# One subtraction of 2048 columns on GpSimd where there were four of 512

## The reference

```python
for layer in range(2):
    h = _rmsnorm(x, norm_mix[layer])
    if layer == 0:
        q, k, v, g, alr, u, sv = _split(h @ even_w_in[0], EVEN_SPLITS)
        m = concat([_gla(q, k, v, g, alr, ...), _sgu(u, sv, ...)])
        x = x + m @ even_w_out[0]
    else:
        p = h @ odd_w_in[0]
        m = concat([_rwkv7(p[..., :RWKV_IN], ...), _conformer_conv(p[..., RWKV_IN:], ...)])
        x = x + m @ odd_w_out[0]
    f = jnp.square(jax.nn.relu(_rmsnorm(x, norm_ffn[layer]) @ w_up[layer]))
    x = x + f @ w_down[layer]
return _rmsnorm(x, norm_final)
```

## Time and profile before

| | |
|---|---|
| median of 3 runs | 1486.62 us |
| lowest and highest | 1486.29 and 1496.51 us |
| the profiled execution, its own time | 1486.62 us |
| its span in the profile | 1484.8 us |
| TensorE (matmul) busy | 1400.2 us, 94% |
| VectorE busy | 683.8 us, 46% |
| ScalarE busy | 420.8 us, 28% |
| GpSimd busy | 514.5 us, 35% |
| mean granted TensorE clock | 0.954 |

### The profile page before, as it was taken

One profiled execution on the slowest core, in us unless ns is written; L12 is line 12 of the kernel. 1 busy time (PEld: TensorE's weight loads), 2 busy tenths in 40 slices (PEclk: granted clock), 3 DMA queues, 4 the chain that ended last, 5 costly groups with the idle time before them and its releaser, 6 DMA issues. The chain is left out here.

```text
span 1484.8 us, 18004 instructions
## 1 busy us (share of the span) xinstructions
PE 1400.2 (94%) x7124; PEld 1138.8 (77%) x7124; DVE 683.8 (46%) x972; ACT 420.8 (28%) x535; POOL 514.5 (35%) x383
## 2 busy tenths in 40 slices
PE   4999998999999999889999999998799999999997
PEld 3896976888888888668878778686577888888886
DVE  6234356641024412666758677665556430044213
ACT  4545322321122212353324232221323321222210
POOL 3442342554444544241111110110043554454541
PEclk9999998999999999899999996996898999999998
DMA  4320212223223222111010000000021323223221
GB/s 185 125 97 29 74 68 85 85 85 114 85 85 109 88 90 108 57 57 58 1 58 29 29 29 1 29 29 0 0 86 59 111 85 113 85 85 113 85 85 57
DMA packets 16792, 106.01 MB, mean 71 GB/s; under 512 B 1872, under 2 KB 2144, under 8 KB 4704
## 3 DMA queue, kind: packets, MB, share of 16 engines
q1 hardware_dynamic: 15872, 103.83, 19.7%
q10 hardware_dynamic: 864, 1.36, 0.3%
HBM read 103.09 MB, written 2.10 MB: 71 GB/s over the span
## 5 line engine op out<-in xcount | busy, mean ns | idle before, releaser
L411 POOL TENSOR_TENSOR w_lo<-w_raw,w_hi 128x512 fp32r<-128x512 f32 x376 | 509.9, 1386 | 933.6 <-ACT w_hi L477 324.7
L749 PE MATMUL ps<-h_hi,w_hi 128*128 128x512 f32 x792 | 322.2, 407 | 7.9 <-DVE h_lo L1191 4.3
L749 PE MATMUL ps<-h_hi,w_lo 128*128 128x512 f32 x792 | 312.3, 394 | 0.0
L749 PE MATMUL ps<-h_lo,w_hi 128*128 128x512 f32 x792 | 312.2, 394 | 0.0
L749 PEld LDWEIGHTS ps<-h_hi,w_hi 128*128 128x128 f32 x792 | 150.8, 190 | 54.8 <-issue 18.4
L477 ACT ACTIVATE w_hi<-w_raw 128x2048 fp32r<-128x2048 f32 x58 | 111.1, 1915 | 276.5 <-PE ps L749 204.2
L749 PEld LDWEIGHTS ps<-h_hi,w_lo 128*128 128x128 f32 x792 | 150.8, 190 | 32.4
L749 PEld LDWEIGHTS ps<-h_lo,w_hi 128*128 128x128 f32 x792 | 151.1, 191 | 30.9 <-issue 2.2
L1245 DVE TENSOR_TENSOR x<-x,ps 128x512 f32 (+1 forms) x32 | 22.0, 687 | 305.2 <-PE ps L749 233.7
L749 PE MATMUL ps<-f_hi,w_lo 128*128 128x512 f32 x384 | 151.9, 396 | 0.0
L749 PE MATMUL ps<-f_hi,w_hi 128*128 128x512 f32 x384 | 151.9, 396 | 0.0
(11 more groups left out here) (279 smaller groups left out, 1999.4 us busy)
## 6 DMA issues: line engine op xcount, KB each, us to landing
w_raw<-in_weights SPq DMA_DIRECT2D x94, 1024.0 KB, 4.8
outT<-x SPq DMA_DIRECT2D x8, 256.0 KB, 2.2
x<-in_xT ACTq DMA_DIRECT2D x4, 256.0 KB, 6.8
x<-in_xT SPq DMA_DIRECT2D x4, 256.0 KB, 6.2
masks_f<-in_masks SPq DMA_DIRECT2D x1, 768.0 KB, 14.0
low_w<-in_low_w SPq DMA_DIRECT2D x1, 512.0 KB, 14.8
sgu_ln<-in_sgu_ln SPq DMA_DIRECT2D x1, 512.0 KB, 3.6
sgu_w<-in_sgu_w SPq DMA_DIRECT2D x1, 256.0 KB, 3.8
```

Source lines behind the costliest of these rows:

```text
L411: piece = pool.tensor_tensor(w_lo[:, j, at], w_raw[:, j, at], w_hi[:, j, at].bitcast(f32), SUB)
L749: mm = pe.matmul(bank(gb(g) if isinstance(i, int) else g % 2), w, r, start=(k == 0 and m == 0), stop=(k == K - 1 and m == 2))
```

## The change

GpSimd computes the remainder of a chunk with one instruction over all 2048 columns, where it had four instructions of 512 columns each. `lo_done` is raised once per chunk, as it was. No other engine's program changes.

```diff
                 for j in range(2):
 
                     pool.wait_ge(s("hi_done"), 2 * n + (j + 1))
-                    for part in range(4):
-                        at = slice(512 * part, 512 * part + 512)
-                        piece = pool.tensor_tensor(w_lo[:, j, at], w_raw[:, j, at], w_hi[:, j, at].bitcast(f32), SUB)
-                    piece.then_inc(s("lo_done"), 1)
+                    pool.tensor_tensor(w_lo[:, j, :], w_raw[:, j, :], w_hi[:, j, :].bitcast(f32), SUB)\
+                        .then_inc(s("lo_done"), 1)
```

## The result

The changed kernel takes 1500.56 us (median of 20 runs, 1496.79 to 1505.38), the kernel before 1492.92 us over 20 runs of its own (1476.34 to 1498.34). The ratio is 1.0064 with a 95% interval of 1.0042 to 1.0087: slower by 6 to 13 us, 7.6 between the medians. That is within 1% and on the side that was forecast, but more than the 5.5 us forecast, and the median lies 0.56 us above the stated range. In what follows, ratios and times at equal clock leave out the runs that were more than 1.5% above the fastest of their kernel, while medians and ranges hold all runs.

The account below looks back on a forecast made before the run. TensorE, busy 94% of the span, was taken as the bound, with GpSimd reaching its path by holding VectorE out. Terms +1.3 - 0.8 + 2.0 + 3.0 = +5.5 us on 1486.62 gave 1492 us, range 1484 to 1500.

Parts of the forecast that it names:

- A turn kept for the whole instruction: GpSimd and VectorE exclude each other at SBUF, so a merged instruction holds VectorE up to four times as long.
- four VectorE operations in a chunk as the point of indifference: Four or more operations needing the turn lose the same in sum; with fewer, early ones wait for the whole rest.
- the MLP's cover: Upward half, 32 chunks: `f_lo` still ends 1.7 us (0.7 at worst) before its bank is needed; cost 0.
- Rival (a): VectorE gets in between within a long instruction, so every wait stays: 1486.6 us, chance 0.13.
- Rival (b): `Sd` wins its turn at 937 us, the rest goes as forecast: 1488.5 us, chance 0.22.
- Rival (c): Longer TensorE waits in layer 1's mixer lower its clock: slower by over 1%, 1504.6 us at 25 us, chance 0.08.
- The hold: Time a merged GpSimd instruction keeps VectorE out: taken as 4.0 us, bounded by 3.8 and 5.0.
- Norms 1 to 3: All four `diag` wait for the whole subtraction, then TensorE spreads in a row: 0.4 us each, +1.3 for three.
- Norm 0: First chunk lets go earlier, all four `diag` precede the second chunk, `h_lo` ends at 25.0 instead of 25.75: gain 0.8.
- Start of the mixer: Layer 1: `t_c` waits three more holds, delaying `t_d` and the chain behind it; second chunk adds nothing: +2.0 us (1.5 to 4).
- State update: At 937 us `Sd` comes just behind the subtraction and waits three more holds, delaying TensorE's step: +3.0 us (2.8 to 4).
- The MLP and the other chunks: MLP's upward half, layer 1's seven other mixer chunks and layer 0's mixer: cost 0, the mixer chunks within 1 us either way.

Follow-up runs that it names:

- a5: Changed kernel with only chunk 58's subtraction moved behind the `Sd` it blocks: 1495.63 us, ratio to before 1.0014, +5.0 us at equal clock.
- b2: Changed kernel, one instruction per chunk, with six chunks (16, 48, 63, 49, 50, 58) started later, behind VectorE or TensorE steps: 1488.56 us, ratio to before 0.9978.
- a3: Changed kernel with two sets, norm chunks (1, 16, 48, 63) and layer 1's mixer chunks (49 to 59), in four pieces: 1493.07 us, ratio to before 1.0019.
- a0: The changed kernel again as it stands, one instruction per chunk, beside 35 runs of the kernel before: 1503.26 us, ratio 1.0053, +8.0 us at equal clock.

## Why the prediction was wrong

Two steps failed, while the mechanism held. The sum was put on a base, 1486.62 us, that lies 6.3 us below the median of 20 runs. And the sum itself was too small, 5.5 us against 7.6 between the medians, mainly because the hold of a merged instruction was put at 4.0 us (it is 4.28) and because the second chunk of the mixer's start was put at nothing. Of the 8.4 us by which 1486.62 + 5.5 falls short of 1500.56, the base makes 6.3 and the sum 2.1.

**The direction and the mechanism held.** A turn kept for the whole instruction, four VectorE operations in a chunk as the point of indifference (but for the start of the mixer, below), the MLP's cover, `t_c` and `Sd` as the victims: each has its row above. Rival (a), no whole-instruction turn, falls by the maxima of `diag`, `t_c` and `Sd`. Rival (b), that `Sd` wins its race, did not happen in either profile of the merged kernel, and a5 shows what it would have been worth, 3.0 us. Rival (c), the clock, has one row for it. Beside the earlier trace rows:

```profile
850.00:975.00 125.00, 115.48 (x636) 90.81 (x635) 79.82 (x111) 32.63 (x57) 9.09 (x2) 0.81 0.05 18
```

In this one execution the clock of the stretch was 0.81 where it had been 0.88. Over the runs the clocks are 0.9455 and 0.945, so (c) falls as the cause.

**The size was too small**, 5.5 against 8.0 us at equal clock (7.4 to 7.6 between medians). Term by term:

1. *The hold*, taken as 4.0 us "since the beat of the norm is the cleanest row". It is 4.28 by `Sd`. The choice of row failed: 0.94 us came from the beat of 1.22 less the 0.28 that one `diag` takes from start to end. Four `diag` that don't wait take 0.87 us together (b2), so each follows the last by 0.20, and 1.22 - 0.20 is 1.02. The rows of `f_sq`, `diag` and `Sd` themselves (1.0 to 1.1 us added) were the direct measure, and four times those is 4.2. The 94 subtractions last 4.50 to 5.04 us, where 4.1 to 4.6 was expected.
2. *Norms 1 to 3*, forecast 0.4 each (the clock times given there, 246.4 against 245.90, make it 0.5): 0.85, 0.84 and 0.85, that is 2.5 for three as against 1.3. The form of the sum was right (2.06 us for the spread, measured 2.08); VectorE was let in at 244.80, 4.3 us after GpSimd's start, and most of the miss is the hold.
3. *Norm 0*, forecast a gain of 0.8: `h_lo` ended 10.56 us after the first subtraction's start and ends 10.25 after it, a gain of 0.3. The second hold was longer as well.
4. *Start of the mixer*, forecast 2.0: from the end of the scan to the bonus step it was 20.24 us (634.64 to 654.88) and is 22.99 (638.20 to 661.19), +2.75. The reciprocal is 2.2 later, as the chain through `t_d` said. The other 0.6 is the second chunk, costed at nothing "since four operations need the turn". With four waits of up to 1 us against one of more than 3, that rule holds only if all four wait in full before, and `AR` had waited 0.1 (0.81 us for an operation of 0.69).
5. *State update*, forecast 3.0: the wait grew from 0.98 to 3.80, +2.8. Right. (The prediction read `Sd` as long once; in the kernel before it was long a second time, 1.25 us at 840.0, and in the changed kernel that one takes 0.25.)
6. *The MLP and the other chunks*, forecast 0: a3 shows 0 for the 79 chunks outside the two sets.

The terms as measured give 2.5 - 0.3 + 2.75 + 2.8 = 7.8 us, which is the loss within its error. TensorE's own account agrees: after the first matmul its time between matmuls grew from 62.2 to 73.6 us, by 11.4, and the first four norms give 4.1 of that back, since the spread takes 2.08 us of matmuls in one row where it took 2.8 to 3.2. That leaves 7.3 us.

**The base was too low, and the range with it.** The 1486.62 us was the median of three runs of a kernel whose runs go from 1476 to 1498, and over 20 runs that median is 1492.92. The profiled execution, the same 1486.62, had a clock of 0.954, where the 35 runs beside a0 have 0.945 at the median. A forecast of +5.5 us on the base of 20 runs would have been 1498.4. One of the three runs stood 10 us above the others, and I read it as scatter of the clock without asking whether the other two were the scatter.

## What to carry to other kernels

When GpSimd and VectorE both work from SBUF as here, the length of a GpSimd instruction sets the longest time that a VectorE operation is kept out, and it is paid where few such operations stand on a chain that TensorE waits for. Cut the GpSimd work into pieces until it would itself come late, or start it behind the short VectorE step that it would block; look for its price at the handful of meetings on the chain and not in its own busy time. And compare versions at equal granted clock before believing a difference of a few microseconds, with one slope for both and at a clock that both have reached.

## What the runs showed of the hardware

The turn grows by 2.1 ns a column from 128 to 2048 columns of float32 (0.23 to 4.28 us), and a VectorE instruction of 64 columns waits about as long for it as one of 512 (4.28 and 4.41 us, `Sd` and `f_sq`). Splitting costs GpSimd little: a chunk takes 4.61 us in one piece at the median, 4.97 in two, 5.25 in four, 5.92 in eight and 7.63 in sixteen, waits for VectorE included. A piece of 512 columns lasts 1.29 us and keeps VectorE out for 1.04 of them. Operations that read PSUM and one SBUF tile were not held up: in the changed kernel `vT` takes 0.75 us at 651.53, inside a subtraction from 651.30 to 655.88, and `Sp` 0.28 at 742.17, inside one from 740.76 to 745.30. And 0.001 of the mean granted clock went with 1.0 to 1.5 us of time, depending on the version (1.36 for the kernel before), which made 20 us of scatter between runs of one and the same program.
